# Two projection units of the first block moved from the middle attention heads to behind the last head

## The reference, cut to what matters

```python
xn = rms_norm(h, ln_attn_pre[l])
proj = xn @ w_in[l]
y_rwkv = rwkv7_mix(proj[..., :RWKV_COLS], mu_shift[l], ...)
dq, dk, dv = jnp.split(proj[..., RWKV_COLS:], 3, axis=-1)
...
o = diff_attention(dq, dk, dv, lam, slopes)     # two softmaxes a head, combined
o = rms_norm(o, diff_subln[l], eps=SUBLN_EPS) * (1.0 - lam_init)
mix = jnp.concatenate([y_rwkv, o.reshape(B, S, DIFF_DIM)], axis=-1)
h = h + rms_norm(mix @ w_out[l], ln_attn_post[l])
```

## Time and profile before

| | before |
|---|---|
| median of 3 runs | 3418.6 us (3414.34 to 3420.74) |
| the profiled execution | 3410.53 us |
| its span, first to last instruction | 3408.8 us |
| what lies around the span | 1.7 us |
| TensorE matmuls busy | 3125.3 us, 92% of the span |
| VectorE busy | 1580.5 us, 46% |
| ScalarE busy | 972.6 us, 29% |
| mean granted TensorE clock | 0.970 |

### The profile page before, as it was taken

The page is one execution under the profiler, slowest core; times in us unless marked ns, Lnnn a source line. Parts: engine busy times, 40 slices in busy tenths (PEclk is TensorE's granted clock), DMA queues, the critical chain, the costliest instruction groups (busy, mean ns, idle before and its releaser), DMA issues.

```text
span 3408.8 us, 48696 instructions
## 1 busy us (share of the span) xinstructions
PE 3125.3 (92%) x20334; PEld 2511.2 (74%) x20334; DVE 1580.5 (46%) x1882; ACT 972.6 (29%) x1434; POOL 678.1 (20%) x292
## 2 busy tenths in 40 slices
PE   7999958888799999999879999999899999999998
PEld 5877747776667888788748886776578877877776
DVE  3155655552274444444471115545554544445455
ACT  3144434442242222222232114334433311111112
POOL 2311111111241122112134330000012222212120
PEclk9999979998899999999989999999999999999999
DMA  4433320102141111111035443353644411111111
GB/s 169 151 114 100 99 83 25 36 7 70 45 152 45 37 55 49 44 37 55 19 118 157 137 154 97 116 153 104 210 142 136 136 50 50 49 49 44 43 37 62
DMA packets 233976, 292.69 MB, mean 86 GB/s; under 512 B 10057, under 2 KB 182226, under 8 KB 233818
## 3 DMA queue, kind: packets, MB, share of 16 engines
q1 hardware_dynamic: 218842, 243.22, 23.4%
q10 hardware_dynamic: 14976, 47.19, 3.6%
HBM read 209.86 MB, written 80.51 MB: 85 GB/s over the span
## 4 chain that ended last, share of the span: by engine, by line
PE 82%; DVE 8%; issue 4%; ACT 3%; DMA 1%; POOL 1%; SPq 0%; DVEq 0%; ACTq 0%; POOLq 0%
PE ps L357 56%; PE ps L482 6%; PE ps L1690 5%; PE ps L1181 4%; PE ps L1760 2%; PE ps L1741 2%; DVE cb L2267 1%; PE ps L1244 1%; PE ps L1718 1%; DVE y L2177 1%; DVE xl L398 1%; POOL src L2070 1%; PE ps L1721 1%; PE ps L1204 1%; PE ps L1222 1%
## 5 line engine op out<-in xcount | busy, mean ns | idle before, releaser
L334 POOL TENSOR_TENSOR wl<-wraw,wh 128x1024 fp32r<-128x1024 f32 x151 | 368.3, 2439 | 1651.7 <-ACT wh L329 1651.7
L357 PE MATMUL ps<-xh,wh 128*128 128x512 f32 x2192 | 685.7, 394 | 7.1 <-POOL xl L1031 2.2
L357 PE MATMUL ps<-xl,wh 128*128 128x512 f32 x2192 | 677.3, 390 | 0.0
L357 PE MATMUL ps<-xh,wl 128*128 128x512 f32 x2192 | 676.0, 390 | 0.0
L357 PEld LDWEIGHTS ps<-xh,wh 128*128 128x128 f32 x2192 | 411.7, 189 | 104.8 <-DVE xl L398 7.2
L357 PEld LDWEIGHTS ps<-xl,wh 128*128 128x128 f32 x2192 | 413.3, 189 | 86.6
L357 PEld LDWEIGHTS ps<-xh,wl 128*128 128x128 f32 x2192 | 412.4, 188 | 86.3
L329 ACT ACTIVATE wh<-wraw 128x1024 fp32r<-128x1024 f32 x167 | 177.0, 1060 | 970.1 <-PE ps L357 885.9
L2177 DVE TENSOR_TENSOR y<-ps,y 128x1024 f32<-128x1024 f32 x208 | 252.3, 1222 | 254.2 <-PE ps L357 254.2
L2098 POOL TENSOR_TENSOR dl<-draw,dh 128x2048 fp32r<-128x2048 f32 x27 | 128.0, 4739 | 612.5 <-ACT dh L2094 612.5
L357 PE MATMUL ps<-dh,fh 128*128 128x512 f32 x512 | 160.2, 394 | 21.3 <-DVE y L2177 15.5
(11 more groups left out here) (304 smaller groups left out, 4564.6 us busy)
## 6 DMA issues: line engine op xcount, KB each, us to landing
wraw<-in_w_up SPq DMA_DIRECT2D x76, 512.0 KB, 3.9
wraw<-in_w_in SPq DMA_DIRECT2D x67, 512.0 KB, 4.4
draw<-in_w_down SPq DMA_DIRECT2D x27, 1024.0 KB, 5.1
residual<-src ACTq DMA_DIRECT2D x32, 512.0 KB, 4.9
proj<-stage SPq DMA_DIRECT2D x30, 512.0 KB, 3.0
qk_hi<-hs ACTq DMA_DIRECT2D x24, 512.0 KB, 2.8
qk_lo<-ls SPq DMA_DIRECT2D x24, 512.0 KB, 2.9
kh<-qk_hi SPq DMA_DIRECT2D x48, 256.0 KB, 6.9
```

The lines of the kernel that those rows point to most:

```text
L334: nc.gpsimd.tensor_tensor(wl[:, s, :, :], wraw[:, s, :, :], wh[:, s, :, :].bitcast(F32), ALU.subtract).then_inc(w_lo, 1)
L357: mm = nc.tensor.matmul(ps[:, bank + h, :], w, x[:, h * HALF:(h + 1) * HALF], start=start and k == 0, stop=stop and k == 2)
```

## The change

`FOUR1` goes: heads 1 and 2 fill by `THREE1`, 48 matmuls fewer each. `TAIL1` gets the 96 matmuls: 48 behind the last step and 72 behind the two transposes of the head's output. Units then end at steps 3, 5 and 7 of heads 0 to 2 and at steps 3 and 5 of head 3; units 11, 12 and 13 end behind the last head. On ScalarE the root of head 3 goes ahead of the weight split, on VectorE the norm goes ahead of the reading of unit 11, and the splits, reads and shifts of the later units are put behind.

```diff
-        FOUR1 = [[16], [16], [16], [16], [16, 16], [16, 32], [12, 12], [12, 12]]
-        LEAD1, TAIL1 = [12, 12], [24]
-        FILL1 = [[[6], [6], [6], [6], *THREE1[4:]], FOUR1, FOUR1, [*THREE1[:6], [6, 6], [6, 6]]]
+        LEAD1, TAIL1 = [12, 12], [48, 72]
+        FILL1 = [[[6], [6], [6], [6], *THREE1[4:]], THREE1, THREE1, [*THREE1[:6], [6, 6], [6, 6]]]
...
-            ends[HEADS1, 0] = [13]
+            ends[HEADS1, 0] = [11, 12, 13]
...
             fill(TAIL1[0])
             turn_output(HEADS1 - 1, 0)
             turn_output(HEADS1 - 1, 1)
+            fill(TAIL1[1])
             bank_free([])
...
             square(b, TT - 1)
-            split_hi(act, IN_TILES + 1, 1)
             root(b)
+            split_hi(act, IN_TILES - 1, 1)
             output(b, 0)
             output(b, 1)
             store(b)
+            for s in range(2):
+                split_hi(act, IN_TILES + s, s)
...
             output(b, TT - 1)
             shift()
-            evac(13)
             normed(b)
+            evac(11)
             shift()
             low(b, 0)
             low(b, 1)
+            for u in (12, 13):
+                evac(u)
+                shift()
```

## The result

The changed kernel takes 3424.7 us (median of 22 runs, 3417.40 to 3430.62) against 3417.68 us of the kernel before (22 runs beside them, 3405.95 to 3427.20): ratio 1.0022, 95% interval 1.0014 to 1.0030. By the ratio that is 7.5 us more, between 4.8 and 10.3; the two medians differ by 7.0. The predicted time was 3424.5 us. The effect was predicted as +5.9 us, under the 0.2% that were taken as the limit of what can be told; with this many runs it can be told, and lies just over it.

What follows compares the result with a forecast made beforehand. TensorE was taken as the bound (92% of the span), with an 18 us hole behind the last head. Heads -19.9, tail +24.1, loads -0.5 and clock +2.2 gave +5.9 on 3418.6: 3424.5 us, range 3413 to 3432.

Steps and rivals of the forecast that it cites:

- The heads: Heads 1 and 2, filled like head 3 with 48 matmuls fewer each, give back 19.9 us; ends 18.3 and 21.5.
- The tail: Behind the last head, the 96 moved matmuls and three waits of 1.6 us lengthen the tail by 24.1 us.
- D: Distance from the tail fill's first matmul to L497's first, the mixer's start; predicted to grow from 24.0 to 48.1 us.
- T: Start of the tail fill, from which tail times are counted; 446.84 us before, about 425.3 to 427 predicted after.
- The moved splits on ScalarE and GpSimd ... These cost nothing.: In the tail, weight splits (2.44 us the longer) end by T + 37 under the last shift; no cost.
- The clock: New 1.6 us waits in the tail cause 1.4 falls of TensorE's clock in all, +2.2 us; ends 0 and 5.1.
- rival 1: Each of three tail waits drops the clock, 4.8 us in place of 2.2; total +9.0, 3427.6 us; chance 0.40 with other losses.
- The loads of wa and gl: At the tail's end, loads no longer run beside the head's stores; gain 0.5 us, between none and about 1.1.
- E: Last part of D, from the end of the last shift to L497; predicted as an unchanged 10.86 us before the load gain.
- The sum: Whole kernel: -19.9 + 24.1 - 0.5 + 2.2 = +5.9 us, 3424.5 us; no change that can be told, slow side.
- Rival 3: Faster: hole shrinks to 15 us, clock stays at 2.4 GHz into the mixer, giving 3 to 5 us; chance 0.07.

Runs made afterwards that it cites:

- e1: Changed kernel with the old order behind the last head (weight split ahead of root, read of unit 11 ahead of norm); tail fill to L497 50.0 us.
- e2: Changed kernel with GpSimd's last weight split held until the last unit is shifted; ratio to the kernel before 1.0021.
- e3: Changed kernel with units 12 and 13 in accumulator banks of their own and the second output transpose in bank 5; ratio to the kernel before 1.0003.
- e4: Changed kernel with wa, gl and first decay/rate weights loaded ahead of late stores, tanh and sigmoid ahead of the last two weight splits; ratio to before 0.9994.
- e8: Half the change: only head 2 gives up 48 matmuls, 24 ahead of the two transposes and 48 behind; ratio to the kernel before 1.0020.
- e5: Kernel before, nothing moved, with early loads and with tanh and sigmoid ahead of the last weight split; ratios to the kernel before 0.9981 and 0.9985.
- e6: Changed kernel with last GpSimd split held back, own banks and early loads together; ratios to the kernel before 0.9966 and 0.9974.

## Why the prediction was right, point by point

**The heads.** Predicted -19.9, ends 18.3 and 21.5; the traces at equal spells, counted from head 1, give -19.9. Right, and by the steps given: steps 0 to 6 take 43.9 us and the wait of 0.7 us came in head 1. One slip is without effect: the sum is set against the profiled execution "with its own three spells", where the prediction's own count gives four. Reading head 3 as a model for heads 1 and 2 was the step that carried this.

**The tail.** Predicted D 48.1 less 0.5 for gl, 47.6; measured 50.0 on the average of three traces with the changed kernel's tail (50.2, 49.7, e1). e2, in which the last diff_t is undisturbed, has 47.6. So the tail grew by 26.0 us. Every mark in between was met: the norm ended at T + 4.6 (predicted 5.0), unit 12 began at T + 7.1, the second half of its fill at 15.3 (15.1), unit 13 at 22.45 (22.2), the last read at 33.6 (33.4).

**The step that failed: "The moved splits on ScalarE and GpSimd ... These cost nothing."** They are hidden from TensorE, but not from VectorE. Before, the last split (453.78 to 456.12) began as the read ended, ran while VectorE waited for the root and through the first of the scaling, and was over when diff_t began. Afterwards it starts 0.07 us ahead of diff_t, in all six traces with moved units in which it is not held back (the changed kernel twice, e1, e3, e4, e8): both hang on the end of unit 13, the one over VectorE's read of 1.23 us, the other over ScalarE's rounding of 1.06. Price 2.1 us, on the path: the last shift ends at T + 39.6 (predicted 37.2), and at T + 37.45 in e2. The step asked what the moved work costs on its own engine and whether it holds the meeting of the engines, and not beside which engine it can't run.

**The clock.** Predicted +2.2 us for 1.4 spells in the tail; measured none. In the five traces with the three waits (the changed kernel twice, e1, e2, e4) 15 waits of 1.4 and 1.7 us brought no spell. The interpolation between waits of 1.05 and 1.85 us was wrong, and with it rival 1. The rule that the prediction draws from the Trainium skill, "TensorE: Matmul & The Clock Gate", section "A second HAM failure mode: psum-queue depth-cycling", on short idles between groups, is borne out for the heads' 1.85 us and not for these. So the close agreement of the total is partly luck: +2.2 for spells that didn't come stands in the place of +2.1 for the slow diff_t. A second piece of luck is in the absolute time: the three runs of before that it was built on had a median 0.9 us above that of the 22, so 3424.5 and 3424.7 agree better than +5.9 and the measured +7.0 to +7.5.

**The loads of wa and gl.** Predicted -0.5: E is 10.8 us in the two traces of before and 10.3 on the average in the seven traces with moved units and late loads, between 10.06 and 10.65. Right in size; that the head's stores beside gl are the reason was not tested, and in the first trace of each kernel the time from the issue of wa to tanh differs by 0.2 us only.

**The sum.** -19.9 + 26.0 = +6.1 us from the traces, with +7.5 (4.8 to 10.3) and +7.2 (3.4 to 10.9) from the times. The forecast put the effect just inside 0.2%; it lies just over. Rival 1's total, +9.0, is inside the intervals too, but its mechanism, three spells in the tail, didn't come. The heart of the prediction, that the hole hangs on the last unit and is behind it again, held; e4 and e5 show that this bond is an order of stores, loads, tanh and sigmoid that can be changed, wherever the units stand. Rival 3, a clock that stays up over the shorter hole, fell too. TensorE's 4 us stretches of the changed kernel show both, the clock full through the tail's waits and low in the hole:

```profile
432.00:436.00 4.00, 3.38 (x15) 1.00 0.00 0
...
444.00:448.00 4.00, 2.59 (x13) 1.00 0.31 126
...
464.00:468.00 4.00, 0.00 (x0) 0.50 0.53 180
```

## What to carry to other kernels

Work moved into a hole at the end of a stage fills it only if the hole doesn't hang on that work: look at what follows the last piece in its queues, and move that first (the loads, tanh and sigmoid queued behind an unrelated store were worth some 8 us here, the filling in a clean tail 2.5). Filling needs a second buffer as well, or each piece waits for the reading of the one before. And when two engines go on from the same event, ask whether they can run side by side; moving a "hidden" operation changes its neighbour.

## What the runs showed of the hardware that had not been expected

- VectorE's diff_t (two inputs from SBUF) took 3.35 to 3.42 us whenever it started just behind GpSimd's split of 2.4 us, and 1.21 to 1.23 otherwise. In e6, where one split starts as diff_t ends, the stage operation behind it takes 3.34 in place of 1.28 us, as the timeline of that kernel shows. Whether a read of PSUM, with one input from SBUF, would be slowed too is not shown: in no trace does one lie beside a split for more than 0.05 us.

```profile
443.09 1.23 DVE L1450 TENSOR_TENSOR diff_t<-shifted 128x1024 f32<-128x1024 f32 x1
...
444.22 2.40 POOL L334 TENSOR_TENSOR wl<-wraw,wh 128x1024 fp32r<-128x1024 f32 x1 [10.57 <-ACT wh L329]
...
444.35 3.34 DVE L1454 SCALAR_TENSOR_TENSOR stage<-diff_t,cols,shifted 128x1024 f32<-128x1024 f32 x1
```

- Waits of TensorE of 1.85 us for a head's output were followed by a spell of low clock in 44 of 84 cases over 14 traces, each with 1.7 us of lost clock and about 1.45 us of time; waits of 1.41 and 1.66 us in none of 15; the wait of 6.34 us in both of its cases. What in between decides is left open.
- Between two executions of the kernel before the number of spells alone (four and two) moved the start of the tail by 2.9 us. That is about half of what this change is worth, and the one trace from which the prediction was made was one of these two.
